# A decoder layer in fp32r: kept weight halves, stores moved to SyncE, and attention outputs from side-by-side stationary columns

## The reference

```python
hn = rmsnorm(h, g_attn_norm)
z = hn @ w_in                      # 1024 x 1280: q (512), k (128), v (128), u (512)
q, k = per_head_rmsnorm(q, g_q), per_head_rmsnorm(k, g_k)
a = sliding_window_sink_attention(q, k, v, sinks, rel_bias)   # 8 heads of 64, 2 kv heads, window 128
m = multiscale_pool_mixer(u, w_pool, pool_scale)              # trailing means of 2/4/8/16, then 128x128 maps
h = h + concatenate([a, m]) @ w_out                           # 1024 x 1024
hn = rmsnorm(h, g_ffn_norm)
h = h + (silu(hn @ w_gate) * (hn @ w_up)) @ w_down            # hidden width 2816
gate = sigmoid(rmsnorm(h, g_ple_norm) @ w_ple_gate)
h = h + gate * (p @ w_ple_proj)
```

## Time and profile before

| | |
|---|---|
| median of three runs (lowest, highest) | 2105.85 us (2102.95, 2106.06) |
| the profiled execution | 2101.83 us |
| its span, first to last instruction | 2100.0 us |
| busy in the span: TensorE, VectorE, ScalarE, GpSimd | 2060.4, 1386.2, 947.6, 306.3 us |
| z0 and what is before it | 0 to 88 us |
| z1, out0, z2, out1, z3, out2, out3 start at | 88, 175, 228, 322, 373, 467, 540 us |
| the FFN starts at | 593 us |
| last matmul starts at | 2093.1 us |

### The profile page before, as it was taken

The page is one execution under the profiler, slowest core; times in us unless marked ns, Lnnn a source line. Parts: engine busy times, 40 slices in busy tenths (PEclk is TensorE's granted clock), DMA queues, the critical chain, the costliest instruction groups (busy, mean ns, idle before and its releaser), DMA issues.

```text
span 2100.0 us, 26622 instructions
## 1 busy us (share of the span) xinstructions
PE 2060.4 (98%) x9802; PEld 1702.8 (81%) x9802; DVE 1386.2 (66%) x1905; ACT 947.6 (45%) x1528; POOL 306.3 (15%) x450
## 2 busy tenths in 40 slices
PE   6999999999999999999999999999999999999998
PEld 5878778787788888888888888788888888888887
DVE  3576766767696556566688664876556566987653
ACT  3485674677663333333333453533333333333532
POOL 2443333343230000000000010000000000000100
PEclk9999999999999999999999999999999999999999
DMA  7433345343672232233916017632232227442143
GB/s 184 128 80 91 101 106 147 110 131 101 208 232 92 66 108 68 81 96 113 334 60 196 25 51 211 180 102 75 69 108 69 79 97 276 150 157 75 41 130 100
DMA packets 199244, 253.44 MB, mean 121 GB/s; under 512 B 15291, under 2 KB 128612, under 8 KB 197836
## 3 DMA queue, kind: packets, MB, share of 16 engines
q1 hardware_dynamic: 183344, 207.20, 33.6%
q0 software_dynamic: 13248, 42.53, 5.7%
q10 hardware_dynamic: 2524, 2.02, 0.4%
HBM read 203.44 MB, written 49.82 MB: 121 GB/s over the span
## 4 chain that ended last, share of the span: by engine, by line
PE 72%; DVE 1%; issue 0%; DMA 0%; ACT 0%; SPq 0%; POOL 0%; ACTq 0%
PE bank L2390 13%; PE bank L2394 13%; PE bank L2392 13%; PE bank L2452 7%; PE bank L2453 7%; PE bank L2454 7%; PE bank L2079 4%; PE bank L2081 4%; PE bank L2080 4%; PE bank L2107 1%; DMA raw<-in_w_ple_gate 0%; DVE w_lo L1396 0%; PE bank L2416 0%; ACT w_hi L918 0%; DVE a_lo L1693 0%
## 5 line engine op out<-in xcount | busy, mean ns | idle before, releaser
L2390 PE MATMUL bank<-a_hi,ring_hi 128*128 128x512 f32 x1232 | 480.4, 390 | 0.3 <-DVE h_last L1602 0.2
L2394 PE MATMUL bank<-a_hi,ring_lo 128*128 128x512 f32 x1232 | 479.4, 389 | 0.0
L2392 PE MATMUL bank<-a_lo,ring_hi 128*128 128x512 f32 x1232 | 479.3, 389 | 0.0
L2390 PEld LDWEIGHTS bank<-a_hi,ring_hi 128*128 128x128 f32 x1232 | 231.2, 188 | 49.0 <-issue 0.8
L2392 PEld LDWEIGHTS bank<-a_lo,ring_hi 128*128 128x128 f32 x1232 | 231.3, 188 | 48.1
L2394 PEld LDWEIGHTS bank<-a_hi,ring_lo 128*128 128x128 f32 x1232 | 231.2, 188 | 48.0
L2452 PE MATMUL bank<-d_hi 128*128 128x512 f32 x616 | 240.8, 391 | 0.0
L2454 PE MATMUL bank<-d_hi,d_lo 128*128 128x512 f32 x616 | 239.8, 389 | 0.0
L2453 PE MATMUL bank<-d_lo,d_hi 128*128 128x512 f32 x616 | 239.7, 389 | 0.0
L1396 DVE TENSOR_TENSOR w_lo<-raw,w_hi 128x1024 fp32r<-128x1024 f32 x111 | 140.9, 1270 | 143.5 <-ACT w_hi L918 142.5
L1236 ACT ACTIVATE d_hi<-keep 128x1024 fp32r<-128x1024 f32 x132 | 139.7, 1060 | 201.3 <-PE bank L2454 184.2
(11 more groups left out here) (238 smaller groups left out, 3821.0 us busy)
## 6 DMA issues: line engine op xcount, KB each, us to landing
hidden_T<-hid POOLq DMA_DIRECT2D x88, 256.0 KB, 2.3
raws<-in_w_gate SPq DMA_DIRECT2D x84, 256.0 KB, 4.7
raws<-in_w_up SPq DMA_DIRECT2D x84, 256.0 KB, 5.2
raw<-in_w_in SPq DMA_DIRECT2D x78, 256.0 KB, 3.9
keep<-hidden_T SPq DMA_DIRECT2D x66, 256.0 KB, 3.8
raw<-in_w_out SPq DMA_DIRECT2D x64, 256.0 KB, 4.1
raw<-in_w_ple_gate SPq DMA_DIRECT2D x64, 256.0 KB, 4.2
keep<-in_w_down SPq DMA_DIRECT2D x44, 256.0 KB, 4.4
```

The lines of the kernel that those rows point to most:

```text
L2390: mm(dst[:, :], wh[:, g, cols], a_hi[o][:, k, :], start=fresh and k == 0, stop=False, skip_group_check=True)
L2392: mm(dst[:, :], wh[:, g, cols], a_lo[o][:, k, :], start=False, stop=False, skip_group_check=True)
L2394: ins = mm(dst[:, :], wl[:, g, cols], a_hi[o][:, k, :], start=False, stop=k == 3, skip_group_check=True)
```

## The change

- The split halves of the eighteen panels 10 to 27 (z1 and out0) are also stored to DRAM by SP (`store_parts`, two DMAs of 512 KB each, ahead of the next panel's load). For the 44 panels 28 to 71 nothing is split: GpSimd's queue loads both halves (`load_parts`, 1 MB a panel) into one of three slots, two panels ahead.
- `store_n2` goes from GpSimd's queue to SP's.
- `attend` puts the high and the low values of one kv head side by side as 128 stationary columns: eight matmuls of 256 columns instead of six of 512. The high rows hold the product with the high values, the other 64 rows that with the low ones. ScalarE copies the low share into `share` (shifted by 64 rows), VectorE adds the high one (`attn_sum`, which frees bank 6), and then `attention_hi` and `attention_rest` split `share` with one instruction each, at the end of a step.
- Start: SP loads panel 0 behind the four blocks of rows; its split moves behind the sums of squares; the third block is transposed ahead of z0; `constants` moves from half 1 to half 4 and the one-hot matmul from half 3 to half 5.
- In the embedding gate, the panel split at the boundary of the two column halves moves ahead by some instructions. The last 512 columns are finished in two pieces, and the last four blocks of the output are stored by SP instead of GpSimd.
- A wait of the second ring part (m = 1) is for `panel_used` instead of `lo_done`.

```diff
+        vv = sb("vv", [P, 2, 4, HEAD_DIM], RING0 + 2.5, F32R)
...
+        share = sb("share", [P, 2, P], RING0 + 4.5)
...
+        w_parts = [sb(f"w_parts{i}", [P, 2, PANEL], at, F32R) for i, at in enumerate((WRAW, WHI, WLO))]
...
+        def has_parts(i):
+            return SPLIT_END <= i < ROW_PANELS
+        def split_of(i):
+            return min(i, SPLIT_END) + max(i - ROW_PANELS, 0)
+        def parts_slot(i):
+            return (i - SPLIT_END) % SLOTS_W
...
+        def split_behind(second, e, r):
+            return not (e == 1 and (r == 0 or second and r == 3))
+        def drained(n):
+            return [slice(0, T // 2), slice(T // 2, T)] if n == 8 * NT - 1 else [slice(0, T)]
...
+            def store_parts(i):
+                sp.wait_ge(lo_done, i + 1)
+                for part, src in enumerate((panel_hi(i), panel_lo(i))):
+                    sp.dma_start(w_split[i - KEPT_FROM, part], src.bitcast(F32)
+                                 ).then_inc(parts_stored[i % 2], 16)
+            def load_z(t, c):
+                if t < 2:
+                    load(Z_AT[t] + c, z_panel(c))
+                elif t == 2 and c == 0:
+                    store_parts(SPLIT_END - 2)
+                    store_parts(SPLIT_END - 1)
+            def load_out(t, c):
+                if t == 0:
+                    load(OUT_AT[t] + c, out_panel(c))
...
                 elif i >= 2:
-                    sp.wait_ge(lo_done, i - 1)
+                    sp.wait_ge(lo_done, split_of(i) - 1)
+                if KEPT_FROM <= i - 2 < SPLIT_END:
+                    store_parts(i - 2)
                 for dst, src in panel_parts(i, halves):
...
+            def store_n2(t, b, e):
+                n = 8 * t + 2 * b + e
+                sp.wait_ge(n2_copied, n + 1)
+                dst = hnT_d[t // 2, b // 2, :, 4 * e:4 * e + 4, t % 2, (b % 2) * P:(b % 2) * P + P]
+                sp.dma_start(dst, hnT[:, n % 2, :, :]).then_inc(n2_stored[n % 2], 16)
...
+                load(Z_AT[0] + c, z_panel(c))
...
+                    load_z(t + 1, c)
+                    for half in (2 * c - 2, 2 * c - 1):
+                        if t and half in N2_AT:
+                            store_n2(t - 1, *N2_AT[half])
...
+                load_out(3, c)
+                for half in (2 * c, 2 * c + 1):
+                    if half in N2_LAST_AT:
+                        store_n2(2, *N2_LAST_AT[half])
                 if c == 3:
                     load_a(0, 0)
...
+                if half == 0:
+                    for b in range(NB):
+                        for e in range(2):
+                            store_n2(3, b, e)
...
+            for j in range(NB):
+                t, b = late_block(NT - 1, j)
+                for piece, cols in enumerate(drained(8 * (NT - 1) + 4 + j)):
+                    sp.wait_ge(ple_out, 8 * (NT - 1) + 4 + j + piece + 1)
+                    sp.dma_start(out_block(t, b, 1)[:, cols], h2[(NT - 1) % 2][:, j, T + cols.start:T + cols.stop]
+                                 ).then_inc(last_stored, 16)
...
+            def load_parts(i):
+                kept = (10 + i - OUT_AT[1] if OUT_AT[1] <= i < Z_AT[3] else i - Z_AT[2] if i < Z_AT[3] else
+                        i - Z_AT[3] if i < OUT_AT[2] else 10 + (i - OUT_AT[2]) % 8)
+                if i == SPLIT_END:
+                    pool.wait_ge(lo_done, SPLIT_END)
+                elif i < SPLIT_END + SLOTS_W:
+                    pool.wait_ge(panel_used, SPLIT_END)
+                    for parity in range(2):
+                        pool.wait_ge(parts_stored[parity], 16 * (SPLIT_END - KEPT_FROM))
+                else:
+                    pool.wait_ge(panel_used, i - SLOTS_W + 1)
+                pool.wait_ge(parts_stored[kept % 2], 32 * (kept // 2 + 1))
+                for part in range(2):
+                    pool.dma_start(w_parts[parts_slot(i)][:, part, :], w_split[kept, part]
+                                   ).then_inc(parts_landed[parts_slot(i)], 16)
...
+                    if t == 0 and half == 14:
+                        load_parts(Z_AT[2])
+                    if t and half % 2 == 0 and OUT_AT[t] + half // 2 + 2 < ROW_PANELS:
+                        load_parts(OUT_AT[t] + half // 2 + 2)
...
-            pool.wait_ge(out_stored, 128 * NT)
+            pool.wait_ge(out_stored, 128 * NT - 64)
+            pool.wait_ge(last_stored, 16 * (NB + 1))
...
+                    return
+                act.wait_ge(landed[i % 2], 32 * (split_of(i) // 2) + 32)
                 if i >= 2:
                     act.wait_ge(panel_used, i - 1)
+                if KEPT_FROM <= i - 2 < SPLIT_END:
+                    act.wait_ge(parts_stored[i % 2], 32 * ((i - 2 - KEPT_FROM) // 2 + 1))
                 nc.scalar.activation(panel_hi(i), panel_raw(i), ACT.Copy).then_inc(hi_done, 1)
...
+            def attention_share(n, c):
+                if c % 2:
+                    act.wait_ge(pv, n // 2 + 1)
+                    if n // 2:
+                        act.wait_ge(attn_lo, n // 2)
+                    for j in range(2):
+                        last = nc.scalar.activation(share[head_rows(j), :, :], attended(j, 1 - j), ACT.Copy)
+                    last.then_inc(shared, 1)
             def attention_hi(s, n, b, c):
                 if c % 2:
-                    act.wait_ge(pv, n // 2 + 1)
-                    for j in range(2):
-                        last = nc.scalar.activation(mix_of(s)[0][head_rows(j), c - 1:c + 1, bass.ts(b, P)],
-                                                    attended(j), ACT.Copy)
-                    last.then_inc(attn_hi, 1)
+                    act.wait_ge(attn_sum, n // 2 + 1)
+                    nc.scalar.activation(mix_of(s)[0][:, c - 1:c + 1, bass.ts(b, P)], share[:, :, :],
+                                         ACT.Copy).then_inc(attn_hi, 1)
...
+                    attention_share(16 * s + k - LAG_PV, unit(k, LAG_PV)[1])
...
+                if has_unit(k, LAG_PV):
+                    attention_hi(s, 16 * s + k - LAG_PV, *unit(k, LAG_PV))
...
-                    if t == 0 and half == 1:
+                    if t == 0 and half == 4:
...
-                    act.wait_ge(lo_done, ROW_PANELS)
+                    act.wait_ge(panel_used, ROW_PANELS - 1)
...
+                        for cols in drained(n):
+                            nc.scalar.activation(buf[:, cols], bank[(BS1, BS0)[e][b]][:, cols], ACT.Tanh,
+                                                 scale=0.5).then_inc(sig, 1)
+                        if e == 0 and b == 1:
+                            split(ple + 7)
...
-                if b == 1:
-                    split(0)
+                if b == 2:
                     norm_hi(0, bank[4], wide_hi, 0, 0)
                     norm_hi(1, bank[5], wide_hi, 1, 0)
-                if b >= 2:
-                    for e in range(2):
-                        i = 2 * b - 2 + e
-                        norm_hi(i, bank[4 + i % 4], wide_hi, e, b - 1)
+            split(0)
+            for i in range(2, 6):
+                norm_hi(i, bank[4 + i % 4], wide_hi, i % 2, i // 2)
...
+                v = qkv_of(s)[:, b, QKW:].rearrange("p (j d) -> p j d", j=2)
+                hi = vv[:, n % 2, 0:4:3, :]
+                nc.vector.tensor_copy(hi, v).then_inc(v_hi_done, 1)
                 dve.wait_ge(v_hi_done, n + 1)
-                nc.vector.tensor_tensor(v_lo[:, n % 2, :], v, v_hi[:, n % 2, :].bitcast(F32),
+                nc.vector.tensor_tensor(vv[:, n % 2, 1:3, :], v, hi.bitcast(F32),
...
+            def attention_sum(n, c):
+                if c % 2:
+                    dve.wait_ge(shared, n // 2 + 1)
+                    for j in range(2):
+                        at = (head_rows(j), slice(0, 2), slice(0, P))
+                        last = nc.vector.tensor_tensor(share[at], attended(j, j), share[at], ALU.add)
+                    last.then_inc(attn_sum, 1)
             def attention_rest(s, n, b, c):
                 if c % 2:
                     dve.wait_ge(attn_hi, n // 2 + 1)
                     hi, lo = mix_of(s)
-                    for j in range(2):
-                        at = (head_rows(j), slice(c - 1, c + 1), bass.ts(b, P))
-                        last = nc.vector.tensor_tensor(lo[at], attended(j), hi[at].bitcast(F32), ALU.subtract)
-                    last.then_inc(attn_lo, 1)
+                    at = (slice(0, P), slice(c - 1, c + 1), bass.ts(b, P))
+                    nc.vector.tensor_tensor(lo[at], share[:, :, :], hi[at].bitcast(F32),
+                                            ALU.subtract).then_inc(attn_lo, 1)
...
+                    if t == 0 and half == 4:
...
+                    if t == 0 and half == 6:
...
+            def panel_ready(i):
+                if has_parts(i):
+                    pe.wait_ge(parts_landed[parts_slot(i)], 32 * ((i - SPLIT_END) // SLOTS_W + 1))
+                else:
+                    pe.wait_ge(lo_done, split_of(i) + 1)
...
```

(24 more changed lines are left out.)

132 lines of the change are left out of this document (60 added, 72 removed).

## The result

The changed kernel takes 2121.03 us (median; 2117.34 to 2122.29), the kernel before 2105.85. The ratio is 1.0072 (1.0057 to 1.0087): 15 us slower, where I had forecast no change, and above my range of 2090 to 2118. The profiled execution has a span of 2116.8 us, 16.8 more than before.

What follows compares the result with a forecast made beforehand. TensorE, busy 2060.4 of 2100.0 us, was taken as the bound. Terms -14.4 - 6 - 1 - 2.5 + 1 + 13.5 + 6.5 + 2 = -0.9 us gave 2105.0 on the median, range 2090 to 2118.

Steps and rivals of the forecast that it cites:

- Attention times values: Attention stages: eight 256-column matmuls take 1.04 us a pair instead of 1.49; 14.4 us gained over 32 pairs, bounds 3 to 15.
- the chain of copies: Attention steps: the added ScalarE and VectorE copying lies beside TensorE; cost 0, with 0 to +4 us.
- Start: First tile: first real matmul at 17.8 instead of 19.17, no wait before panel 2; 6 us gained, bounds 2 and 8.
- End: After the last matmul: finishing in halves, with SP issuing, gains 1 us, bounds 0 and 2.
- The panel split that moves ahead in the last stages: Last stages: moving this split ahead removes no wait of TensorE; 0 us.
- Kept halves: Panels no longer split: 2.5 us gained from earlier attention work (bounds 8 and -3), 1 us lost to traffic (0 to 6).
- Entry of the FFN: Stores on SP delay loads: first product 13.5 us (bounds 8 and 20), then a second wait 6.5, clock 2.
- the second wait: FFN entry, fourth product: the last tile's row stores stand behind `load_pair(0,1)`; TensorE 6.5 us later, bounds 0 and 9.
- the clock term: FFN entry: long idle stretches let TensorE's clock fall; 2 us lost, bounds 0 and 5.
- rival 2: Kept panels come late because GpSimd issues them in order; 1 us for some 15 panels, sum +14, 2120; chance 0.15.
- Rival 3: Attention: weight loads pace the short matmuls, gain 3 instead of 14.4 us; sum +10.5, 2116; chance 0.05.
- ScalarE's new waits show up as TensorE waits: Attention stages, TensorE waits for `share`: a sign that the prediction is wrong in kind; no size given.

Runs made afterwards that it cites:

- the deferral: High copy and subtraction of each pair of units one attention step later: changed kernel 2116.42 us (1.0056); kernel before with the short matmuls alone 2105.74 us (0.9997).
- old_pv: Changed kernel with attention times values as before (six 512-column matmuls per pair, two copies, two subtractions): 2121.85 us, 1.0077 to the kernel before.
- pv_alone: Kernel before with only the short matmuls and their copies added: 2113.17 us, 1.0035 to the kernel before.
- kept_alone: Kernel before with only the kept weight halves added (stored once, loaded by GpSimd): 2101.74 us, 0.998 to the kernel before.
- pv_alone_deferred: Kernel before with the short matmuls alone, high copy and subtraction one attention step later: 2105.74 us, 0.9997 to the kernel before.

## Why the prediction was wrong, point by point

**Attention times values: the term that failed.** Size and spacing of the matmuls were right (1.03 us a pair, 14.8 us in all). The sentence that failed is "on the path since TensorE paces these stages", with "I take 0 for it, with 0 to +4" for the chain of copies. In the changed kernel what comes back is 14 us, in the kernel before with this edit alone 23. I had argued by ScalarE's busy time (66 of 88 us in the densest tile), a mean over a stage. What counts, as far as the deferral shows it, is the order of waits within a step: a second crossing from ScalarE to VectorE and back, with the softmax and low-part steps of later units queued behind. The row that should have warned me is in my own groups: at 396.35 TensorE waits 1.69 us for VectorE *before* the change. I had booked such waits as 2.5 us to be won by the kept halves. At that place the changed kernel has 2.15 us, at the other that I named (251.5) it has

```profile
250.80 0.30 PE L2235 MATMUL bank<-ident,qkn 128*128 128x128 f32 x1 [0.37 <-DVE probsT_lo L1606]
```

Waits of this kind, for `probsT_lo`, come to 3.4 us before, to 1.2 with the rest of the change and the long matmuls (old_pv), and to 3.0 with the short ones: the kept halves do shorten them, and the short matmuls lengthen them again.

**Start: right to panel 2, then lost.** 5.9 us at panel 2 (forecast 6; but the forecast had the one-hot matmul, 0.8, ahead of panel 2, and it now comes behind), though the first matmul came at 19.40, not 17.8. By the second z 3.2 were left.

**End:** 0.8 for 1. But "The panel split that moves ahead in the last stages has no wait to remove: 0" and "From 600 to 2090 us TensorE never waits" are false. The timeline of the kernel before has

```profile
1330.19 0.50 PE L2079 MATMUL bank<-w_hi,hn_hi_second 128*128 128x512 f32 x1 [2.52 <-DVE w_lo L1396]
```

and no execution with the moved split has it (those of pv_alone, kept_alone and pv_alone_deferred, without it, have 2.78, 2.45 and 2.44). In the changed one, waits of 0.69 and 1.02 near 1369 and 1397 us took most of it back.

**Kept halves: better than priced.** I gave them 2.5 less 1. They bring 4.6 alone and 6.4 beside the short matmuls. The late panel at the start of the third z is there as described (1.62 us). Not foreseen: a block of x for tile 2 lands late behind the stored halves (TensorE waits 1.72 us at 205.68), and the last output stage.

**Entry of the FFN: right mechanism, too small.** Forecast 13.5 + 6.5 + 2 = 22; measured 4.68 + 9.48 + 7.89 = 22.05 of waits and 5.3 of all else, mostly slower matmuls, 27.3. The 12 to 15 us that I placed at the first product came in two pieces; the second wait was 7.9 for 6.5; the clock term of 2 was less than half of what it should have been, though its upper bound was 5. One working was off: 5.2 MB at 355 to 400 GB/s, issued from 570.7, land between 583.8 and 585.4, not between 580.5 and 587; the 583.5 that I took is near the lower end. I assumed that one queue keeps its order; moving two stores ahead of the loads removed 7.5 of 7.9 us, which agrees. So does the Trainium skill ("DMA: Bandwidth & Descriptors", Queues, rings and completion order), which has the descriptors of each ring taken in order, though it lets a later one finish its write first.

**The rivals.** None was the case. The number was near rival 2 (2120), but late kept panels cost 1.6 us, not 15. Rival 3 (2116) had the gain of the edit at 3 for a reason that isn't there: the short matmuls are not paced by their weight loads. The missing rival was the chain on ScalarE and VectorE as the new pace of the attention stages. I had it as a phrase in the last paragraph ("ScalarE's new waits show up as TensorE waits") and no price. With the 14 us that came back, the sum is 13 and the time 2119; that this lands so near 2121 is partly luck, since the entry cost 5 us more than its terms and the kept halves gave 3 to 5 more than theirs.

## What to carry to other kernels

Price an edit that shortens TensorE's work by the waits that are already in that stage: where TensorE waits for another engine, count the gain only as far as the chain of that engine isn't lengthened by the same edit, and write out who waits for whom in one step, crossings included. When an in-order queue gets new instructions that wait, list everything behind them, and move the loads ahead rather than the stores elsewhere first. An edit that is worth nothing alone (short matmuls: -7 to 0 us) can be worth 7 us when the engine that it burdens has been relieved and the hand-over deferred by a step.

## What the runs showed of the hardware

Three waits of TensorE of 5 to 9 us cost about a quarter more than their length here: 22 us of waits and 27.3 us of delay, with a granted clock of 0.83, 0.80 and 0.77 in the ten-microsecond windows that follow them (580, 600 and 630 us). A store of 256 KB issued behind 3 MB of loads on the same queue was waited for until 8.7 us after its issue, where the 32 such stores of the changed kernel land in 2.7 at the median.
